# First expert's rows taken from a one-hot of ranks, second expert at a fixed place

## The chip, the cores and the metric

The kernel runs on one core of one Trainium2 chip, in float32 throughout. The metric is the device time of one execution in microseconds (us), the median of several. In the text PE is TensorE, DVE is VectorE, ACT is ScalarE, POOL is GpSimd and SP is SyncE, which issues most of the DMAs.

## The reference

One step of a hybrid decoder layer: 256 prompt rows and 32 sample rows, 288 in all, of width 2048, pass a mixer (gated MLP heads beside sparse attention), a cross-attention into 256 memory tokens, and a mixture of experts. The change is in the last part only:

```python
def hier_moe(n, w_group, b_group, w_router, b_router, w_gate, w_up, w_down):
    xf = n.reshape(B * T, D)
    g_prob = softmax(xf @ w_group + b_group); g_sel = argmax(g_prob)        # 4 groups
    e_logits = (xf @ w_router + b_router) ... [g_sel]                       # 4 experts in the group
    top_w, top_i = lax.top_k(softmax(e_logits), 2)
    top_w = top_w / sum(top_w) * g_gate
    expert_id = g_sel * 4 + top_i
    for e in range(16):
        h = silu(xf @ w_gate[e]) * (xf @ w_up[e])                           # 2048 -> 512
        y = y + combine[:, e:e + 1] * (h @ w_down[e])                       # 512 -> 2048
```

Routed on the reference's inputs, 288 rows pick 576 experts: 21 21 21 19 44 37 50 69 33 36 56 47 28 24 39 31 rows for experts 0 to 15.

## The kernel before, in words

The mixer and the attention take the first 740 us or so. Then the router's logits are computed, the rows are routed, and the experts run one after another.

**Lots and ring.** An expert's weights are six lots of 2.10 MB (128 partitions x 4096 floats): gate and up for the first half of the contraction, gate and up for the second, and two halves of down. The 16 experts make 96 lots, here numbered 0 to 95. They lie in a ring of nine buffers (`ring_at`). SP issues lot n once the semaphore `moe_free` says n + 1: the first nine places come free as earlier stages leave their memory (increments of PE at L1158 to L1220), each later one when PE has read the lot that lies there. PE adds two after the first half of gate and up (products 0 to 7 of 16), two after the second half, and one after each half of down. So lots 9 and 10 wait for the first half of the first expert's gate products.

**Order of the experts.** The expert at place 0 is always expert 0. The others are ranked by how many rows they got (`rnk`, L2313 to L2316): ten take full blocks of 64 rows (`CAP`), the fullest gets a strip of 32 rows more, and the five least filled are light and have 32 rows (`STRIP`) each. Whatever does not fit goes to overflow blocks behind the last expert, which load their expert's six lots again. The order is known when `hot_ready` is 3; SP waits for it ahead of lot 6 (L543) and reads the expert's number from `ids_order`.

**From the router to the first expert.** PE turns the normed rows back (L1210), ACT lays them in `hx` (L1871), POOL writes them to DRAM (`nsc`, L622). PE sums the picks to ranks and counts (L1216, L1218), DVE works out block and place of each pick (L2313 to L2341) and two one-hots (`blk_hot`, `row_hot`), PE multiplies these to tables of slots (`slot_table`, L1227, once for the row numbers and once for weights and scales), DVE turns the first into row addresses (`tabS`), POOL gathers block 0 from DRAM by them (L629), PE turns it (`rows_t`, L1244), DVE lays it as `XT` (`lay_rows`, L2392), and the gate products start (L1292). While it waits, PE does products that nobody reads (`keep_clock`, L1233). SP also holds lot 7 until block 0 has been gathered. Block p + 1 is gathered into the other of two buffers and turned right behind the gate products of expert p.

**One full expert on PE:** 32 gate and up products (64 records in the trace, since each float32 product is two), silu on ACT (L1882), its product with the up half on DVE (L2417), a turn (L1367), a copy on ACT (L1887), 16 down products (L1374), and between them the products that put the expert before back to its rows (`combine`, L1253 and L1257).

Of the kernel before, what the change touches and what calls it, by code (L numbers as in the profile page):

```python
# [37 lines left out]
NEARLY = 2  # L38
NFULL = NEXP - NLIGHT
# [79 lines left out]
def decode_step(nc, consts, buckets, x_prompt, x_sample, cache_k, cache_v, cache_idx_k, cache_mem_k,  # L119
# [5 lines left out]
    with ctx:  # L125
# [316 lines left out]
        row_hot = SQ[:, 0:6 * CAP].rearrange("p (n r) -> p n r", n=6)  # L442
        blk_tab = SQ[:, 6 * CAP:6 * (CAP + 3 * NBLK)].rearrange("p (n b) -> p n b", n=6)
# [28 lines left out]
        fuller = pairs[:, 64:64 + 225].rearrange("p (e f) -> p e f", e=15)  # L472
# [35 lines left out]
        def _(sp):  # L508
# [31 lines left out]
            for e in range(NEXP):  # L540
                expert = e
                if e == 1:
                    sp.wait_ge(S("hot_ready"), 3)  # L543
                if e:
                    expert = sp.value_load(ids_order[:, e:e + 1], min_val=0, max_val=NEXP - 1)
                for i, (wv, part) in enumerate(LOTS):
                    lot = NL * e + i
                    sp.wait_ge(S("moe_free"), lot + 1)
                    if lot == 4:
                        sp.wait_ge(S("stored_mv0"), 16)  # L550
                    if lot == 7:
                        sp.wait_ge(S("xg_in0"), 16)
                    sp.dma_start(ring_at[lot % NRING], lot_of(wv, expert, part)).then_inc(S(f"moe_in{lot % NRING}"), 16)
# [20 lines left out]
        def _(pool):  # L574
# [71 lines left out]
        def _(pe):  # L646
# [568 lines left out]
            for at, lhs, a, z in ((0, "rank", 0, 48), (16, "ones", 0, 32), (32, "ones", 0, 16)):  # L1215
                mm(PS[:, 5, at:at + z - a], cc(lhs), AS[:, :, :].rearrange("p t e -> p (t e)")[:, a:z], start=at == 0, stop=at == 32)  # L1216
            for t in range(3):
                last = mm(PS[:, 5, 48:64], cc("ones"), AS[:, t, :], start=t == 0, stop=t == 2)  # L1218
            last.then_inc(S("rank_ready"), 1)
            pe.nop().then_inc(S("moe_free"), 2)  # L1220
# [157 lines left out]
            def down(landed, bank=4):  # L1378

                for q in range(2):  # L1380
                    w = landed(4 + q).rearrange("p (f n) -> p f n", f=2)
# [31 lines left out]
            def block_rows_t(b):  # L1413

                pe.wait_ge(S(f"xg_in{b % 2}"), 16 * (b // 2 + 1))
                if b:
                    pe.wait_ge(S("xt_laid"), b)
                rows_t(b % 2).then_inc(S("xt_ready"), 1)

            keep_clock(5)  # L1420
            block_rows_t(0)
            def gap(p):

                return lambda s: combine_step(COMBINED_IN[p], s) if p in COMBINED_IN and s < 4 else None
            for p in range(NEXP):
# [75 lines left out]
        def _(act):  # L1501
# [374 lines left out]
            A(RX, RX, ACT.Exp).then_inc(S("r_exp"), 1)  # L1876

# [60 lines left out]
        def _(dve):  # L1938
# [323 lines left out]
            own(V.memset(small[:, 352:416], 0.0))  # L2262
            own(TT(sooner, bc(cc("iota_e")[:, 0:4], 1, [128, 4, 4]), bc(cc("iota_e")[:, 0:4], 2, [128, 4, 4]), ALU.is_lt))
# [46 lines left out]
            dve.wait_ge(S("rank_ready"), 1)  # L2310
# [3 lines left out]
            each = [128, 15, 15]  # L2314
            own(TT(fuller, bc(fill[:, 1:16], 1, each), bc(fill[:, 1:16], 2, each), ALU.is_gt))
            own(V.tensor_reduce(rnk[:, 1:16], fuller, AXX, ALU.add))  # L2316
            own(TS(s32[:, 1:16], rnk[:, 1:16], 0.0, float(STRIP), ALU.is_equal, ALU.mult))
            own(TS(l32[:, 1:16], rnk[:, 1:16], float(NFULL - 1), float(CAP - STRIP), ALU.is_ge, ALU.mult))
            own(TS(later[:, 1:16], rnk[:, 1:16], float(PSTAR), float(CAP + STRIP), ALU.is_ge, ALU.mult))
# [21 lines left out]
            own(TS(ids_slot, ids_slot, CAP - 1, None, ALU.bitwise_and))  # L2341
            own(TT(blk_hot, bc(cc("iota_r")[:, 0:NBLK], 1, [128, 6, NBLK]), bc(ids_blk, 2, [128, 6, NBLK]), ALU.is_equal))
# [5 lines left out]
            by_token(blk_tok, cc("tok")).then_inc(S("hot_ready"), 1)  # L2348
# [9 lines left out]
            dve.wait_ge(S("tab_sum"), 1)  # L2358
            own(TS(tabS[:, :], PS[:, 7, 0:NBLK], 2.0, cc("half"), ALU.mult, ALU.add))
            V.tensor_copy(tabF[:, 0:NBLK], PS[:, 7, 0:NBLK]).then_inc(S("tab_ready"), 1)  # L2360
# [4 lines left out]
            dve.wait_ge(S("tab_sum"), 2)  # L2365
            own(V.tensor_copy(tabF[:, NBLK:3 * NBLK], PS[:, 4, 0:2 * NBLK]))
# [154 lines left out]
```

## Time and profile before

| | us |
|---|---|
| median of 3 runs | 1245.52 (1244.75 to 1247.62) |
| span of the profiled execution | 1242.8 |
| PE busy in it | 1162.2 (94%) |
| DVE busy | 471.6 (38%) |
| ACT busy | 192.8 (16%) |
| mean rate of the DMAs | 264 GB/s over the span |

The profiled execution is one of its own, beside the three that were timed; the page gives its span, from the first to the last instruction. That is 2.7 us under the median of the timed runs, which also hold what lies around the span. A busy PE is not PE at its peak: matmuls are pipelined, and they run at either of two granted clocks, 1.00 (2.4 GHz) and 0.50 (1.2 GHz).

### The profile page before, as it was taken

To read this page: it belongs to the slowest core of one execution; us is meant where nothing else is said; L and a number is where in the kernel's file an instruction comes from. 1 tells how busy PE (TensorE), PEld (TensorE's weight loads), DVE (VectorE), ACT (ScalarE), POOL (GpSimd) and SP (SyncE) were. 2 spreads that over 40 slices of the span, in tenths; PEclk is the share of its full clock that TensorE was granted. 3 is DMA by queue.
4 is the path that set the end of the run, shared out by engine and by line. 5 is a ranking of instruction groups with operands and counts; after the bars stand their busy time and mean duration, and the time that the engine had idled before them with its cause. 6 is when DMAs were issued, how large, how long until landed. Compare 5 with 4: busy or idle time off the path is not lost.

```text
span 1242.8 us, 14135 instructions
## 1 busy us (share of the span) xinstructions
PE 1162.2 (94%) x5878; PEld 569.7 (46%) x5878; DVE 471.6 (38%) x963; ACT 192.8 (16%) x405; POOL 49.6 (4%) x64
## 2 busy tenths in 40 slices
PE   7999999899999998999999899999999999869975
PEld 4334343344444455577777565333333333333332
DVE  5000166079745655011112465233333333412342
ACT  2112233300122234100012422000000000000000
POOL 0002000000000013100001001000000000000000
PEclk9999999999999999899999998999999999979897
DMA  8835532445333348853345636999999999999995
GB/s 288 305 125 144 154 102 87 152 151 179 123 123 102 107 155 321 321 164 136 136 159 187 269 123 251 422 428 425 428 425 427 426 427 428 425 427 428 425 428 220
DMA packets 71229, 327.85 MB, mean 264 GB/s; under 512 B 14108, under 2 KB 17980, under 8 KB 54588
## 3 DMA queue, kind: packets, MB, share of 16 engines
q1 hardware_dynamic: 55152, 282.65, 57.9%
q0 software_dynamic: 8032, 37.23, 8.0%
q10 hardware_dynamic: 7980, 7.05, 2.3%
q8 instruction: 48, 0.79, 0.3%
q14 instruction: 17, 0.14, 0.0%
HBM read 319.04 MB, written 10.49 MB: 265 GB/s over the span
## 4 chain that ended last, share of the span: by engine, by line
PE 79%; DVE 9%; DMA 6%; ACT 3%; ACTq 1%; issue 1%; DVEq 0%; SPq 0%
PE PS L712 20%; PE PS L1019 15%; PE PS L1292 13%; PE PS L1374 6%; DMA ring<-in_w_up 5%; PE PS L1253 4%; PE PS L685 3%; PE PS L1299 2%; DVE X L2038 2%; DVE top L2037 2%; PE PS L1351 1%; PE PS L830 1%; PE PS L1257 1%; PE PS L1003 1%; PE PS L1367 1%
## 5 line engine op out<-in xcount | busy, mean ns | idle before, releaser
L712 PE MATMUL PS<-ring,NC 128*128 128x512 f32 x704 | 322.6, 603 | 1.6 <-issue 1.6
L712 PEld LDWEIGHTS PS<-ring,NC 128*128 128x128 f32 x704 | 129.3, 192 | 154.4 <-issue 152.8
L1019 PE MATMUL PS<-NC,ring 128*128 128x288 f32 x768 | 189.9, 407 | 1.6 <-DVE X L2195 0.5
L1292 PE MATMUL PS<-ring,NC 128*64 128x512 f32 x560 | 163.4, 605 | 8.6 <-DMA ring<-in_w_up 7.2
L1019 PEld LDWEIGHTS PS<-NC,ring 128*128 128x128 f32 x768 | 144.6, 190 | 42.4 <-issue 2.1
L2378 DVE TENSOR_TENSOR X<-X,PS 128x1024 f32<-128x1024 f32 x52 | 63.5, 1221 | 119.2 <-PE PS L1253 119.2
L1292 PEld LDWEIGHTS PS<-ring,NC 128*64 128x64 f32 x560 | 46.3, 138 | 102.4 <-issue 100.8
L1253 PE MATMUL PS<-XNN,NC 64*128 64x512 f32 x208 | 59.0, 644 | 1.4 <-DVE XNN L2422 0.8
L1882 ACT ACTIVATE NC<-PS,small 64x512 f32<-64x512 f32 x11 | 7.5, 682 | 306.7 <-PE PS L1292 272.7
L1299 PE MATMUL PS<-ring,NC 128*32 128x256 f32 x384 | 37.2, 455 | 16.8 <-DMA ring<-in_w_up 13.3
L2195 DVE TENSOR_TENSOR X<-X,PS 128x288 f32<-128x288 f32 x16 | 7.3, 454 | 117.5 <-PE PS L1019 117.5
L2037 DVE MAX8 top<-X 32x8 f32<-32x1028 f32 (+2 forms) x48 | 44.7, 931 | 1.0
L2038 DVE MATCH_REPLACE8 X<-top,X 32x1028 f32<-32x1028 f32 (+2 forms) x48 | 43.9, 914 | 0.0
L2381 DVE TENSOR_TENSOR X<-X,PS 32x1024 f32<-32x1024 f32 x26 | 31.5, 1210 | 26.7 <-PE PS L1257 26.6
L2064 DVE TENSOR_TENSOR ring<-small,cst 64x256 f32<-64x256 f32 x1 | 0.4, 417 | 102.8 <-ACT small L1613 102.8
L1374 PE MATMUL PS<-ring,NC 128*64 128x512 f32 x176 | 39.3, 594 | 0.0
L685 PE MATMUL PS<-ring,NC 128*32 128x512 f32 x288 | 38.4, 605 | 0.0
L1299 PEld LDWEIGHTS PS<-ring,NC 128*32 128x32 f32 x384 | 18.6, 129 | 35.8 <-issue 31.5
L1253 PEld LDWEIGHTS PS<-XNN,NC 64*128 64x128 f32 x208 | 15.9, 187 | 39.5 <-issue 25.6
L2422 DVE COPY XNN<-PS 128x1024 f32<-128x1024 f32 x11 | 13.5, 1225 | 49.8 <-PE PS L1374 37.2
L2417 DVE SCALAR_TENSOR_TENSOR NC<-PS,small,NC 64x512 f32<-64x512 f32 x11 | 8.3, 756 | 50.9 <-ACT NC L1882 50.9
L629 POOL DMA_INDIRECT NC<-nsc,tabS x14 | 14.0, 998 | 340.2 <-PE PS L1244 295.4
(447 smaller groups left out, 1229.1 us busy)
## 6 DMA issues: line engine op xcount, KB each, us to landing
ring<-in_w_gate SPq DMA_DIRECT2D x27, 2048.0 KB, 22.8
ring<-in_w_up SPq DMA_DIRECT2D x22, 2048.0 KB, 20.7
ring<-in_w_in SPq DMA_DIRECT2D x36, 1024.0 KB, 5.1
ring<-in_w_down SPq DMA_DIRECT2D x16, 2048.0 KB, 21.2
ring<-in_w_out SPq DMA_DIRECT2D x16, 1024.0 KB, 5.0
nine<-in_w_down SPq DMA_DIRECT2D x6, 2048.0 KB, 25.6
XNN<-in_w_up SPq DMA_DIRECT2D x5, 2048.0 KB, 22.3
NC<-in_w_gate SPq DMA_DIRECT2D x5, 2048.0 KB, 23.7
```

The source lines that it names most:

```text
L629: nc.gpsimd.indirect_dma_start(xg[:, buf, :], None, nsc.rearrange("t (h d) -> (t h) d", h=2), bass.IndirectOffsetOnAxis(ap=tabS[:, b:b + 1 ...
L685: last = mm(acc(n, 2)[32 * k:32 * k + 32, 0:width], lhs[:, 4 * q + k, T:NT], ws[:, k, 0:width], start=st, stop=sp_)
L712: last = mm(acc(n, t)[:, 0:width], lhs[:, kt, t * 128:(t + 1) * 128], slot(m)[:, k, 0:width], start=kt == 0, stop=kt == KT - 1)
L1019: last = mm(PS[:, j, 0:NT], slot(m)[:, k, 128 * j:128 * j + 128], src[:, kt, :], start=kt == 0, stop=kt == width * 4 - 1)
L1253: last = mm(PS[:, banks + half, :], slot_w[rows, k, 128 * t:128 * t + 128], ysb[rows, k, 512 * x:512 * x + 512], start=True, stop=True)
L1292: last = mm(PS[64 * half:64 * half + 64, 2, :], x[:, kt % 8, kt // 8, :], weights[half][:, kt % 8, :], start=kt == 0, stop=kt == KT - 1)
L1299: last = mm(PS[32 * c:32 * c + 32, bank, 0:256], x[:, kt % 8, kt // 8, STRIP * sub:STRIP * sub + STRIP], weights[c // 2][:, kt % 8, 256 * ...
L1374: last = mm(PS[64 * half:64 * half + 64, bank + x, :], hT[:, f, :], w[:, f % 2, half * 1024 + x * 512:half * 1024 + x * 512 + 512], start= ...
L2037: own(V.max(best, work))
L2038: own(V.match_replace(work, best, work, TAKEN))
L2378: return TT(out, out, PS[:, banks:banks + 2, :], ALU.add)
L2381: last = TT(out, out, PS[32 * x:32 * x + 32, banks:banks + 2, :], ALU.add)
```

## The change

Block 0 is no longer gathered. As soon as the ranks are there, DVE compares each row's rank in expert 0 with 0 to 63 (`hot0`; rows not routed to expert 0 get a rank of 512 or more), and PE multiplies this one-hot with the rows in `hx`: 12 products of 512 columns. ACT copies the result to `xg`, and it is turned and laid as a gathered block was. The tables of slots are built in one pass of 66 columns, inside the gate products of expert 0, ahead of product 8. Block 1 is gathered from these tables and turned between the two halves of expert 0's down products. Expert 1 always has place 1 (`NFIXED`), 14 experts are ranked, and SP waits for the order ahead of lot 12 in place of lot 6. The wait ahead of lot 7 is gone.

```diff
+NFIXED = 2
@@ sync
-                if e == 1:
+                if e == NFIXED:
                     sp.wait_ge(S("hot_ready"), 3)
-                if e:
+                if e >= NFIXED:
                     expert = sp.value_load(ids_order[:, e:e + 1], min_val=0, max_val=NEXP - 1)
-                    if lot == 7:
-                        sp.wait_ge(S("xg_in0"), 16)
@@ gpsimd
-            for b in range(NBK):
-                if b == 1:
-                    pool.wait_ge(S("xg_in0"), 16)
+            for b in range(1, NBK):
                 if b >= 2:
                     pool.wait_ge(S("xt_ready"), b - 1)
                 block_rows(b, b % 2, f"xg_in{b % 2}")
@@ tensor
-            keep_clock(8)
-            pe.wait_ge(S("hot_ready"), 1)
-            slot_table(7, 0, NBLK).then_inc(S("tab_sum"), 1)
-            pe.wait_ge(S("hot_ready"), 2)
-            slot_table(4, NBLK, 3 * NBLK).then_inc(S("tab_sum"), 1)
+            pe.wait_ge(S("row_out"), 12)
+            pe.wait_ge(S("hot_ready"), 1)
+            for x in range(2):
+                for t in range(3):
+                    for half in range(2):
+                        at = half * 1024 + x * 512
+                        last = mm(PS[64 * half:64 * half + 64, 2 + x, :], hot0[0:ROWS[t], t, :], hx[0:ROWS[t], t, at:at + 512],
+                                  start=t == 0, stop=t == 2)
+                last.then_inc(S("route_sum"), 1)
+            keep_clock(1)
...
-            keep_clock(5)
             block_rows_t(0)
+            keep_clock(1)
+            def tables(s):
+                if s == 2:
+                    pe.wait_ge(S("hot_ready"), 2)
+                    slot_table(7, 0, 3 * NBLK).then_inc(S("route_sum"), 1)
...
                     gate_up(lots_at(p), gap(p))
-                    block_rows_t(p + 1)
+                    if p:
+                        block_rows_t(p + 1)
...
-                    down(lots_at(p))
+                    down(lots_at(p), between=(lambda: None) if p else (lambda: block_rows_t(1)))
@@ scalar
             A(RX, RX, ACT.Exp).then_inc(S("r_exp"), 1)
+            for x in range(2):
+                act.wait_ge(S("route_sum"), x + 2)
+                A(xg[:, 0, 512 * x:512 * x + 512], PS[:, 2 + x, :], ACT.Copy).then_inc(S("row_out"), 1)
+            act.wait_ge(S("tab_ready"), 2)
@@ vector
+            own(TS(passed0, AS[:, :, 0], -float(EMPTY), float(EMPTY), ALU.mult, ALU.add))
+            dve.wait_ge(S("route_sum"), 1)
+            own(TT(rank0, rank[:, :, 0], passed0, ALU.add))
+            TT(hot0, bc(cc("iota_r"), 1, [128, 3, CAP]), bc(rank0, 2, [128, 3, CAP]), ALU.is_equal).then_inc(S("hot_ready"), 1)
...
+            own(STT(rnk[:, ranked], rnk[:, ranked], 0.0, rnk[:, ranked], ALU.is_gt, ALU.add))
...
             own(TS(ids_slot, ids_slot, CAP - 1, None, ALU.bitwise_and))
+            dve.wait_ge(S("xt_ready"), 1)
+            lay_rows().then_inc(S("xt_laid"), 1)
             own(TT(blk_hot, ...))
...
+            dve.wait_ge(S("route_sum"), 4)
+            TS(tabS[:, :], PS[:, 7, 0:NBLK], 2.0, cc("half"), ALU.mult, ALU.add).then_inc(S("tab_ready"), 1)
+            V.tensor_copy(tabF, PS[:, 7, 0:3 * NBLK]).then_inc(S("tab_ready"), 1)
```

The instructions of PE from the ranks to the second half of expert 0's down products, before (x8 and the like count instructions of one shape):

```order
L1218 MATMUL PS<-mkT,cst 128x16 x3
L1233 MATMUL PS<-cst 128x512 x8
L1227 MATMUL PS<-SQ 64x22 x12
L1227 MATMUL PS<-SQ 64x44 x12
L1233 MATMUL PS<-cst 128x512 x5
L1244 MATMUL PS<-cst,NC 128x128 x8
L1292 MATMUL PS<-ring,NC 64x512 x32
L1244 MATMUL PS<-cst,NC 128x128 x8
L1367 MATMUL PS<-cst,NC 128x64 x4
L1374 MATMUL PS<-nine,NC 64x512 x8
L1374 MATMUL PS<-ring,NC 64x512 x8
```

and the same stretch of the changed kernel (its L1231, L1225, L1247, L1295, L1370 and L1377 are the L1233, L1227, L1244, L1292, L1367 and L1374 of before):

```order
L1217 MATMUL PS<-mkT,cst 128x16 x3
L1238 MATMUL PS<-X,natS 64x512 x12
L1231 MATMUL PS<-cst 128x512
L1247 MATMUL PS<-cst,NC 128x128 x8
L1231 MATMUL PS<-cst 128x512
L1295 MATMUL PS<-ring,NC 64x512 x16
L1225 MATMUL PS<-SQ 64x66 x12
L1295 MATMUL PS<-ring,NC 64x512 x16
L1370 MATMUL PS<-cst,NC 128x64 x4
L1377 MATMUL PS<-nine,NC 64x512 x8
L1247 MATMUL PS<-cst,NC 128x128 x8
L1377 MATMUL PS<-ring,NC 64x512 x8
```

The 24 table products left the place ahead of the first turn, 12 wider ones stand in the middle of the gate products, and the turn of block 1 went from ahead of L1367 into the down products.

SP's issues of lots 5 to 12, before:

```order
L553 DMA ring<-in_w_down 128x4096 [waits moe_free]
L545 TENSOR_LOAD ids [waits hot_ready]
L545 ISA x2
L553 ISA [waits moe_free]
L553 DMA ring<-in_w_gate 128x4096
L553 DMA XNN<-in_w_up 128x4096 [waits xg_in0,moe_free]
L553 ISA [waits moe_free]
L553 DMA NC<-in_w_gate 128x4096
L553 DMA ring<-in_w_up 128x4096 [waits moe_free]
```

and of the changed kernel:

```order
L553 DMA ring<-in_w_down 128x4096 [waits moe_free]
L553 DMA ring<-in_w_gate 128x4096 [waits moe_free]
L553 DMA XNN<-in_w_up 128x4096 [waits moe_free]
L553 DMA NC<-in_w_gate 128x4096 [waits moe_free]
L553 DMA ring<-in_w_up 128x4096 [waits moe_free]
L553 DMA ring<-in_w_down 128x4096 [waits moe_free] x2
L547 TENSOR_LOAD ids [waits hot_ready]
```

The load of the order moved from ahead of lot 6 to behind lot 11, and lots 6 to 8 wait for nothing but their buffers.

ACT behind its exponential, before:

```order
L1876 ACTIVATE mkT<-mkT 128x15 [waits r_shifted]
L1882 ACT_TABLE_LOAD
L1882 ACTIVATE NC<-PS,small 64x512 [waits moe_free]
L1887 ACTIVATE NC<-PS 128x256 [waits ht_ready]
L1882 ACTIVATE NC<-PS,small 64x512 [waits moe_free]
```

and of the changed kernel:

```order
L1893 ACTIVATE mkT<-mkT 128x15 [waits r_shifted]
L1896 ACTIVATE NC<-PS 128x512 [waits route_sum] x2
L1903 ACT_TABLE_LOAD [waits moe_free]
L1903 ACTIVATE NC<-PS,small 64x512 [waits tab_ready]
L1908 ACTIVATE NC<-PS 128x256 [waits ht_ready]
```

Two copies came in, and the load of the silu's table now carries the wait for `moe_free` that the silu carried.

## Rows read from the trace of the kernel before

**Rows 1.** The page's slices: GB/s that the DMAs moved, 40 slices of the span.
```profile
GB/s 288 305 125 144 154 102 87 152 151 179 123 123 102 107 155 321 321 164 136 136 159 187 269 123 251 422 428 425 428 425 427 426 427 428 425 427 428 425 428 220
```

**Rows 2.** Chain that ended last, around the twelfth expert: start, us, what.
```profile
1081.82 36.03 DMA ring<-in_w_up
...
1117.99 3.68 PE PS L1292 x8
```

**Rows 3.** Stages: us, each engine's busy time (instructions), PEclk, DMA share, GB/s.
```profile
743.00:755.00 12.00, 12.00 (x86) 9.60 (x86) 9.68 (x42) 7.77 (x15) 1.59 (x3) 1.00 1.01 382
755.00:766.60 11.60, 10.06 (x55) 6.97 (x54) 7.30 (x33) 0.00 (x0) 1.08 (x1) 0.73 0.04 10
766.60:784.00 17.40, 15.98 (x59) 6.94 (x61) 4.83 (x19) 0.00 (x0) 2.00 (x2) 0.88 0.99 404
784.00:790.00 6.00, 6.00 (x29) 2.02 (x26) 0.00 (x0) 0.15 (x1) 0.00 (x0) 1.00 0.99 400
...
829.00:858.00 29.00, 28.85 (x136) 10.00 (x134) 10.85 (x10) 1.06 (x2) 1.00 (x1) 1.00 1.01 427
```

**Rows 4.** SP's issues in order of time: lots 5, 6, 9, 15 and 21.
```profile
742.10 0.33 SPq L553 DMA_DIRECT2D ring<-in_w_down  x1
...
766.06 0.36 SPq L553 DMA_DIRECT2D ring<-in_w_gate  x1
...
782.93 0.33 SPq L553 DMA_DIRECT2D ring<-in_w_up  x1
...
809.27 0.33 SPq L553 DMA_DIRECT2D ring<-in_w_up  x1
...
838.47 0.33 SPq L553 DMA_DIRECT2D ring<-in_w_up  x1
```

**Rows 5.** Instructions from the router to the first expert: start, us, engine, line, shapes.
```profile
744.54 5.46 PE L1210 MATMUL PS<-cst,XNN 128*128 128x128 f32 x48
...
745.23 5.86 ACT L1871 ACTIVATE X<-PS 128x512 f32<-128x512 f32 x12 [1.65 <-PE PS L1210]
...
750.51 0.82 PE L1218 MATMUL PS<-mkT,cst 128*128 128x16 f32 x6
...
751.37 0.17 DVE L2313 SCALAR_TENSOR_TENSOR mkT<-PS,cst 128x16 f32<-128x16 f32 x1
...
751.58 0.39 DVE L2315 TENSOR_TENSOR mkT<-mkT 128x225 f32<-128x225 f32 x1
751.59 1.28 ACT L1882 ACT_TABLE_LOAD   x1
...
758.36 0.17 DVE L2341 TENSOR_SCALAR ids<-ids 128x6 int32<-128x6 int32 x1
...
759.84 7.08 PE L1227 MATMUL PS<-SQ 128*64 128x22 f32 x48 [1.54 <-DVE SQ L2347]
...
764.65 1.08 POOL L629 DMA_INDIRECT NC<-nsc,tabS  x1 [12.74 <-issue]
...
773.12 1.28 PE L1244 MATMUL PS<-cst,NC 128*128 128x128 f32 x9
774.54 1.23 DVE L2392 TENSOR_TENSOR NC<-PS,gcol 128x1024 f32<-128x1024 f32 x1 [7.39 <-PE PS L1244]
...
775.82 13.95 PE L1292 MATMUL PS<-ring,NC 128*64 128x512 f32 x64 [1.42 <-DVE NC L2392]
```

**Rows 6.** ACT and PE behind the first gate products, columns as in rows 5.
```profile
789.85 0.68 ACT L1882 ACTIVATE NC<-PS,small 64x512 f32<-64x512 f32 x1 [36.98 <-PE PS L1292]
...
792.87 3.65 PE L1374 MATMUL PS<-nine,NC 128*64 128x512 f32 x16 [0.47 <-ACT NC L1887]
```

**Rows 7.** Stages around the table products, columns as in rows 3.
```profile
759.80:760.80 1.00, 0.96 (x10) 0.90 (x10) 0.86 (x5) 0.00 (x0) 0.00 (x0) 0.82 0.00 0
...
766.80:770.40 3.60, 3.60 (x6) 1.51 (x5) 0.20 (x1) 0.00 (x0) 1.01 (x1) 0.50 1.00 336
```

**Rows 8.** The 14 gathers of blocks: us from issue to landing.
```profile
DMA to landing us min/median/max: 3.4/10.7/12.0
```

More of the change, by code:

```diff
@@ L1215, in _ @@
             for at, lhs, a, z in ((0, "rank", 0, 48), (16, "ones", 0, 32), (32, "ones", 0, 16)):
-                mm(PS[:, 5, at:at + z - a], cc(lhs), AS[:, :, :].rearrange("p t e -> p (t e)")[:, a:z], start=at == 0, stop=at == 32)
+                last = mm(PS[:, 5, at:at + z - a], cc(lhs), AS[:, :, :].rearrange("p t e -> p (t e)")[:, a:z], start=at == 0, stop=at == 32)
+            last.then_inc(S("moe_free"), 2)
             for t in range(3):
                 last = mm(PS[:, 5, 48:64], cc("ones"), AS[:, t, :], start=t == 0, stop=t == 2)
-            last.then_inc(S("rank_ready"), 1)
-            pe.nop().then_inc(S("moe_free"), 2)
+            last.then_inc(S("route_sum"), 1)
             def slot_table(bank, a, z):
@@ L1233, in keep_clock @@
                     mm(PS[:, 6, :], ident, cst[:, 128:640], start=True, stop=True)
-            keep_clock(8)
+            pe.wait_ge(S("row_out"), 12)
             pe.wait_ge(S("hot_ready"), 1)
-            slot_table(7, 0, NBLK).then_inc(S("tab_sum"), 1)
-            pe.wait_ge(S("hot_ready"), 2)
-            slot_table(4, NBLK, 3 * NBLK).then_inc(S("tab_sum"), 1)
+            for x in range(2):
[4 more added lines that the diff above has]
+                                  start=t == 0, stop=t == 2)
+                last.then_inc(S("route_sum"), 1)
+            keep_clock(1)
             def rows_t(k):
@@ L1376, in down_products, with down @@
                 return last
-            def down(landed, bank=4):
+            def down(landed, bank=4, between=lambda: None):
                 for q in range(2):
+                    if q:
+                        between()
                     w = landed(4 + q).rearrange("p (f n) -> p f n", f=2)
@@ L1413, in block_rows_t @@
             def block_rows_t(b):
-                pe.wait_ge(S(f"xg_in{b % 2}"), 16 * (b // 2 + 1))
                 if b:
+                    pe.wait_ge(S(f"xg_in{b % 2}"), 16 * ((b + 1) // 2))
                     pe.wait_ge(S("xt_laid"), b)
+                else:
+                    pe.wait_ge(S("row_out"), 14)
                 rows_t(b % 2).then_inc(S("xt_ready"), 1)
-            keep_clock(5)
             block_rows_t(0)
+            keep_clock(1)
[3 more added lines that the diff above has]
+                    slot_table(7, 0, 3 * NBLK).then_inc(S("route_sum"), 1)
             def gap(p):
+                if p == 0:
+                    return tables
                 return lambda s: combine_step(COMBINED_IN[p], s) if p in COMBINED_IN and s < 4 else None
@@ L2262, in _ @@
             own(V.memset(small[:, 352:416], 0.0))
+            own(V.memset(rnk[:, 1:NFIXED], 1.0))
             own(TT(sooner, bc(cc("iota_e")[:, 0:4], 1, [128, 4, 4]), bc(cc("iota_e")[:, 0:4], 2, [128, 4, 4]), ALU.is_lt))
@@ L2308, in _ @@
             TT(RX[:, :, 0:4], LG[:, :, 0:4], bc(r_max, 2, [128, 3, 4]), ALU.subtract).then_inc(S("r_shifted"), 1)
-            dve.wait_ge(S("rank_ready"), 1)
+            own(TS(passed0, AS[:, :, 0], -float(EMPTY), float(EMPTY), ALU.mult, ALU.add))
+            dve.wait_ge(S("route_sum"), 1)
             rank = PS[:, 5, 0:48].rearrange("p (t e) -> p t e", t=3)
             count = PS[:, 5, 48:64]
+            own(TT(rank0, rank[:, :, 0], passed0, ALU.add))
+            TT(hot0, bc(cc("iota_r"), 1, [128, 3, CAP]), bc(rank0, 2, [128, 3, CAP]), ALU.is_equal).then_inc(S("hot_ready"), 1)
             own(STT(fill, count, 32.0, cc("iota_e"), ALU.mult, ALU.add))
[L2314 to L2319, printed above, removed]
+            ranked, each = slice(NFIXED, NEXP), [128, NEXP - NFIXED, NEXP - NFIXED]
+            own(TT(fuller, bc(fill[:, ranked], 1, each), bc(fill[:, ranked], 2, each), ALU.is_gt))
+            own(V.tensor_reduce(rnk[:, ranked], fuller, AXX, ALU.add))
+            own(STT(rnk[:, ranked], rnk[:, ranked], 0.0, rnk[:, ranked], ALU.is_gt, ALU.add))
+            own(TS(s32[:, ranked], rnk[:, ranked], 0.0, float(STRIP), ALU.is_equal, ALU.mult))
+            own(TS(l32[:, ranked], rnk[:, ranked], float(NFULL - 1), float(CAP - STRIP), ALU.is_ge, ALU.mult))
+            own(TS(later[:, ranked], rnk[:, ranked], float(PSTAR), float(CAP + STRIP), ALU.is_ge, ALU.mult))
             own(STT(limit, s32, float(CAP), l32, ALU.add, ALU.subtract))
@@ L2347, in by_token @@
                 return TT(per_pick(out), per_pick(blk_hot), ap.unsqueeze(1).unsqueeze(3).broadcast_to(x), ALU.mult)
-            by_token(blk_tok, cc("tok")).then_inc(S("hot_ready"), 1)
+            own(by_token(blk_tok, cc("tok")))
             own(by_token(blk_rs, xrs))
@@ L2357, in _ @@
             own(STT(at_place, s32[0:1, :], PSTAR / STRIP, at_place, ALU.mult, ALU.add))
-            dve.wait_ge(S("tab_sum"), 1)
-            own(TS(tabS[:, :], PS[:, 7, 0:NBLK], 2.0, cc("half"), ALU.mult, ALU.add))
-            V.tensor_copy(tabF[:, 0:NBLK], PS[:, 7, 0:NBLK]).then_inc(S("tab_ready"), 1)
             own(TT(who, bc(at_place, 1, [1, 16, 16]), bc(cc("iota_e", 1), 2, [1, 16, 16]), ALU.is_equal))
@@ L2364, in _ @@
             V.tensor_copy(ids_order, at_place).then_inc(S("hot_ready"), 1)
-            dve.wait_ge(S("tab_sum"), 2)
-            own(V.tensor_copy(tabF[:, NBLK:3 * NBLK], PS[:, 4, 0:2 * NBLK]))
+            dve.wait_ge(S("route_sum"), 4)
+            TS(tabS[:, :], PS[:, 7, 0:NBLK], 2.0, cc("half"), ALU.mult, ALU.add).then_inc(S("tab_ready"), 1)
+            V.tensor_copy(tabF, PS[:, 7, 0:3 * NBLK]).then_inc(S("tab_ready"), 1)
+            dve.wait_ge(S("tab_ready"), 2)
             dve.wait_ge(S("iota_in"), 16)
```

11 lines of the change are left out of this document (5 added, 6 removed).

## The prediction

> **What bounds the kernel now.** I read the slices first, then the chain that ended last, then the stages, then SP's issues, and single instructions last. In the slices the last third is level at 425 to 428 GB/s [rows 1]: while the experts run, the DMAs are full. The chain says the same from the other side: at the first strip expert it goes through a weight lot issued at 1081.82 that PE could use only 36 us later [rows 2]. Yet in the full experts PE has no gap either: 28.85 of 29.00 us [rows 3]. Both are near their limit there. SP's issues for one lot of successive experts are 29.2 us apart (809.27 and 838.47) [rows 4], while six lots of 2.10 MB with some 0.4 MB of gathered rows take 13.0 / 0.427 = 30.4 us at the rate of that stage [rows 3]. So PE runs ahead by 1.2 us per expert until the ring is empty of landed lots, and what sets the end is when the stream of lots gets going and how often it stops. An idle DMA before the last lot counts one for one; an idle PE counts only if it starves the stream of free buffers.
>
> The stream has a hole: 11.6 us at 10 GB/s from 755.0 to 766.6 [rows 3]. It ends with lot 6 at 766.06 [rows 4], the first that waits for the order of experts. Behind it the rate is 404 and 400 GB/s up to 790 [rows 3], and from there on full. The changed kernel closes this hole. The question is whether buffers come free in time, since lots 9 to 15 need the gate and down products of expert 0 and the start of expert 1.
>
> **Part 1, the start of the gate products.** Ranks and counts are summed at 750.51 + 0.82 = 751.33, and the gate products start at 775.82 [rows 5]. In place of this: DVE does one small operation ahead of the wait, one behind it (0.17 each, 0.2 with the gap) and the one-hot of 192 elements, by the 0.39 of L2315's 225 [rows 5]: 752.2. The 12 products with 64 weight columns are 24 records; 64 such records took 13.95 us, 0.218 each [rows 5], so 5.2: 757.4. ACT's second copy is a twelfth of 5.86, 0.5 [rows 5]: 757.95. One idle product, by four of those records 0.9, hides it: 758.3. The turn is 1.3 [rows 5]: 759.6. DVE must by then be through with ids_slot: it was at 758.53 [rows 5], and three small operations and the one-hot add 1.0, which gives 759.5, just in time; every 0.1 more there is 0.1 on the path. XT is laid in 1.23 [rows 5], so the gate products start at 761.0, 14.8 us earlier.
>
> **Part 2, expert 0 on PE.** Half of the gate products, 7.0, are done at 768.0. The table pass is 24 records: ten of them took 0.96 us while the clock was still mostly high [rows 7], 48 took 7.08 mostly at the low clock [rows 5]; that is 2.3 to 3.5, and I take 2.4, as PE is warm there. It needs the one-hots, some 2.7 us of DVE behind XT, about 763.7, and is hidden; the order of experts follows at about 765.7 and is needed by SP for lot 12 at 777. The gate products end at 761.0 + 13.95 + 2.4 = 777.35. Now the silu's table: its load took 1.28 at 751.59, with ACT idle [rows 5]. In the changed order this load carries the wait for `moe_free`, so it stands behind the gate products: +1.3 (nothing, if the load gets ahead after all). From the end of the gate products to the down products it was 792.87 - 789.77 = 3.1 [rows 5, 6]: 781.75. The turn of block 1 no longer fills this time, so PE idles 2.9 us there. An idle time of 1.54 ahead of L1227 [rows 5] was followed by a fall of the granted clock, and then 3.6 us of wide products at 0.50 [rows 7]. So I charge the first down half 3.5 + 2.0 (bounds 0 and 3.5): 787.25. The turn of block 1 costs 1.4 in the open, the second half 3.5: expert 1 starts at 792.15, against 792.87 + 7.0 = 799.9, 7.8 earlier. Of the 14.8 us PE gives back 2.4 to tables, 1.3 to the silu's table, 2.0 to the clock, 1.4 to the turn.
>
> Block 1's gather: tables are summed at 768.0 + 2.4 = 770.4, DVE and POOL bring the issue to about 772, the median gather lands 10.7 later and the slowest 12.0 [rows 8]: 782.7 to 784. It is needed at 787.25, or at 785.2 without the fall of the clock. It waits for nothing else, as block 2 uses the other buffer.
>
> **Part 3, the stream.** From 743 to 755 the DMAs moved 4.58 MB [rows 3]: lot 5, the rows written to `nsc` (2.36 MB) and a little; at 427 that is 10.7 us, so starting costs up to 1.3. The changed kernel issues lots 5 and 6 at 742.1 to 742.5 and 7 and 8 at 751: with them 10.9 MB, 25.5 us from 744.3, so 769.8. Lots 9 and 10 are issued at 768.0, in time: with two gathers (21 rows for expert 1, 0.8 us for both) 780.4. Lots 11 and 12, issued at 777.4: 790.2. Lot 13, issued at 787.25: 795.1. Lot 14, at 792.15, and a gather: 800.9. Lot 15 needs the first half of expert 1, which took 809.27 - 799.9 = 9.3 [rows 4, 6]: issued at 801.5. The stream runs dry here; with 1.5 us from issue to full flow (0.9 to 2.2) lot 15 begins at 803.0. From there each expert brings DMA 1.2 us more than PE needs, and it stays full.
>
> Before, lot 15 began after lots 6 to 14 and three gathers, 19.6 MB or 46.0 us from 766.6, plus 0.9 and 0.4 for the two stages below 427 [rows 3]: 813.9. The difference is 10.9 us, and behind lot 15 both kernels move the same lots. The other edits cost nothing: the memset stands ahead of the router beside PE's products, one tensor_scalar fewer ranks 14 in place of 15, SP has one load of the order less.
>
> The Trainium skill, "DMA: Bandwidth & Descriptors", section Specifications, gives about 0.6 us to the first byte for DMAs that SP issues. By that the restart at lot 15 would be 0.9 us shorter, and the time 0.9 lower; the row of 743 to 755 gives more, and I follow the row.
>
> **The sum.** Against its own execution: span 1242.8 - 10.9 = 1231.9; the median of the timed runs lies 2.7 above that span, so 1245.5 - 10.9 = **1234.6**. Own range: at best neither the silu's table nor the clock costs, lot 15 is issued at 798.2, and the full stream sets its start at 799.9 to 801.0: 14.0 gained, 1231.5. At worst within the mechanism, the dear table pass (1.1), the dear clock (1.5) and the slow restart (0.7): 1237.9.
>
> **Rivals.** (a) *The clock falls ahead of the first rows.* PE waits 0.9 us for the one-hot behind narrow products and then runs wide ones. The 24 records at half speed cost between 1.8 (3.6 us at 0.50, as behind L1227 [rows 7]) and 5.2; lot 15 is later by as much: 1236.4 to 1239.8. Against it: from 743 to 755, turns and narrow products included, the clock was 1.00 [rows 3]. The Trainium skill speaks for it ("TensorE: Matmul & The Clock Gate", Part 4: transposes do not count as PE-busy in the same way, so 5.46 us of them would leave the clock low). The trace disagrees so far, as the products right behind them ran at 1.00.
> (b) *PE becomes the bound.* If PE and not the stream sets the end, only its 7.8 us arrive: 1237.7. For it: no gap in the full experts. Against it: the 36 us wait [rows 2].
> (c) *A new wait on the gather.* In the changed kernel six lots are queued when block 1 is gathered. If it lands 16 to 20 us after its issue, PE and lot 14 are late by 1 to 5: 1236 to 1239. No gather took over 12.0 [rows 8].
> (d) *An overflow block: slower.* With expert 1 fixed at a full block, the five light ones are the least filled of 2 to 15, so expert 15 comes in, with 31 rows by the reference's inputs against a strip of 32. From 33 rows on there is an overflow block: six lots more, 6 x 4.9 = 29.5 us, behind the last expert, with nothing beside them: 1264. The counts speak against it.
> (e) *The hole was free anyway.* If the rate late in the stream falls by what comes earlier, nothing is gained. Only the level 425 to 428 speaks, and against it.
>
> **How the numbers follow.** Forecast 0.60, (a) 0.20, (b) 0.07, (c) 0.05, (d) 0.03, (e) 0.05. What this kernel's measurement can tell from no change is 0.2%, 2.5 us, so faster means under 1243.0. Forecast, (a), (b) and (c) lie there: 0.92; (e) is no change, with 0.04 of its 0.05; (d) and the rest slower: 0.04. The range of 8 in 10 takes the forecast's and reaches through (a) to (c): 1231.0 to 1240.0.
>
> **What would show it.** Right, if the gate products start at 760 to 762; if the rate holds near 427 from 744 to 770 with no stretch under 50 GB/s; if ACT's table load stands behind 777 with 2.5 to 3 us of PE idle and a half clock in the first down products; if the second expert's gate products start near 792; and if lot 15 is issued near 801.5 after a short dip. Wrong, if the hole only moves (lots 9 and 10 issued past 772), if the gather releases the turn of block 1, or if the wait at the first strip expert is gone, since then PE sets the end.

## The result, and the profile after

The changed kernel took 1237.82 us (median of 5, 1233.77 to 1239.22) against 1245.52 (also of 5, 1244.75 to 1247.62). The medians lie 7.7 us apart; the ratio is 0.9922 with a 95% interval of 0.9902 to 0.9942, so 7 to 12 us were gained. The forecast was a gain of 10.9 us and a time of 1234.6. In the profiled execution the span was 1236.5 and the time 1239.10.

The first thing to see in that trace is that lot 5 is issued at 747.09 and not at 742.10 as before [rows 4], though nothing ahead of it was changed but one small memset. Here are SP's issues in the changed kernel (start, us, what; lots 5 to 10 and 15, the pair 10 and 11 in one row):

```profile
747.09 0.33 SPq L553 DMA_DIRECT2D ring<-in_w_down  x1
747.46 0.43 SPq L553 DMA_DIRECT2D ring<-in_w_gate  x1
...
755.70 0.33 SPq L553 DMA_DIRECT2D XNN<-in_w_up  x1
756.07 0.65 SPq L553 DMA_DIRECT2D NC<-in_w_gate  x1
773.70 0.33 SPq L553 DMA_DIRECT2D ring<-in_w_up  x1
774.07 9.35 SPq L553 DMA_DIRECT2D ring<-in_w_down  x2
...
807.83 0.33 SPq L553 DMA_DIRECT2D ring<-in_w_up  x1
```

So I count from the issue of lot 5. T is the time from there to the end of the span: 1242.8 - 742.1 = 500.7 before, 1236.5 - 747.1 = 489.4 after. Lot 9 went from 40.8 behind lot 5 to 26.6, lot 15 from 67.2 to 60.7, the last lot, 95, from 454.5 to 445.0. PE is 6.5 us earlier at lot 15, the stream of lots 9.5 us earlier at its end, and the tail behind the last issue is 1.8 shorter (44.4 in place of 46.2). That makes T 11.3 shorter.

The tail's part has nothing to do with the stream: the last expert's down products ran at the full clock in this trace and in part at the half clock before (start, us; the first two rows are of the changed kernel, the last two of the kernel before):

```profile
1220.06 1.92 PE L1354 MATMUL PS<-nine,NC 128*32 128x512 f32 x16 [0.48 <-ACT NC L1913]
1221.77 1.93 PE L1354 MATMUL PS<-ring,NC 128*32 128x512 f32 x16
...
1224.84 3.50 PE L1351 MATMUL PS<-nine,NC 128*32 128x512 f32 x16 [0.43 <-ACT NC L1892]
1228.15 1.91 PE L1351 MATMUL PS<-ring,NC 128*32 128x512 f32 x16
```

That is 1.6 of the 1.8 us.

The stages of the changed kernel (us, each engine's busy time, PEclk, DMA share, GB/s) answer to [rows 3]:

```profile
760.00:765.00 5.00, 5.00 (x25) 2.32 (x24) 3.62 (x18) 1.19 (x2) 0.00 (x0) 1.00 1.02 431
785.00:790.00 5.00, 3.51 (x11) 1.65 (x13) 0.76 (x1) 0.55 (x2) 0.00 (x0) 0.53 1.00 422
795.00:805.00 10.00, 10.00 (x44) 2.87 (x43) 3.64 (x3) 0.00 (x0) 0.99 (x1) 1.00 0.99 415
805.00:810.00 5.00, 5.00 (x24) 1.56 (x24) 2.31 (x2) 0.00 (x0) 0.00 (x0) 1.00 0.82 311
810.00:829.00 19.00, 18.85 (x94) 7.08 (x90) 7.32 (x8) 1.06 (x2) 0.99 (x1) 1.00 0.97 393
829.00:858.00 29.00, 28.85 (x135) 10.01 (x134) 10.66 (x10) 1.06 (x2) 0.99 (x1) 1.00 1.01 429
```

The hole is gone: 431 GB/s where it had been. Ahead of that, while the rows' write to DRAM was on its way, the rate was not near 427 as forecast but 340 GB/s from 747 to 755 and 375 to 760. What is left is a shortfall around lot 15, where the forecast had the stream run dry: against 427 GB/s the rows from 795 to 829 lack 0.3, 1.4 and 1.5 us (length times the missing share). Most of the last 1.5 is a second, smaller dip right behind the issues of lots 17 and 18 (817.25 and 818.35), with 1.2 us missing:

```profile
818.00:824.00 6.00, 5.85 (x34) 2.58 (x35) 3.82 (x4) 0.38 (x1) 0.99 (x1) 1.00 0.90 340
```

The clock is at 0.53 from 785 to 790, where PE had waited for the silu.

The instructions of the route answer to [rows 5, 6] (start, us, engine, line, shapes, idle before):

```profile
757.14 5.81 PE L1238 MATMUL PS<-X,natS 128*64 128x512 f32 x24 [0.81 <-DVE natS L2337]
...
763.85 1.32 PE L1247 MATMUL PS<-cst,NC 128*128 128x128 f32 x9
...
765.31 1.23 DVE L2370 TENSOR_TENSOR NC<-PS,gcol 128x1024 f32<-128x1024 f32 x1 [1.10 <-PE PS L1247]
...
766.59 7.09 PE L1295 MATMUL PS<-ring,NC 128*64 128x512 f32 x32 [0.56 <-DVE NC L2370]
...
773.51 2.55 PE L1225 MATMUL PS<-SQ 128*64 128x66 f32 x24
...
783.19 1.28 ACT L1903 ACT_TABLE_LOAD   x1 [19.59 <-PE PS L1295]
...
786.01 1.07 PE L1370 MATMUL PS<-cst,NC 64*128 64x64 f32 x5 [2.94 <-DVE NC L2442]
...
787.56 5.92 PE L1377 MATMUL PS<-nine,NC 128*64 128x512 f32 x16 [0.47 <-ACT NC L1908]
```

The reader is to see the silu's table loaded behind the gate products, the 2.94 us of idle PE that follow, and the first down half at 5.92 us in place of 3.65 [rows 6].

The chain that ended last still waits for a lot at the first strip expert, as in [rows 2]:

```profile
1078.73 35.20 DMA ring<-in_w_up
```

### The profile page after: what moved, and what is told of

Same layout as the page of the kernel before. It is cut to its first block, busy times and chain, and to the rows that moved or that the text cites. A ratio compares the mean times of both kernels' runs of the same rounds, so it can differ in the third digit from the quotient of the medians.

```text
span 1236.5 us, 14083 instructions
## 1 busy us (share of the span) xinstructions
PE 1153.0 (93%) x5856; PEld 561.8 (45%) x5856; DVE 472.6 (38%) x967; ACT 194.1 (16%) x407; POOL 48.7 (4%) x63
## 4 chain that ended last, share of the span: by engine, by line
PE 79%; DVE 8%; DMA 6%; ACT 3%; ACTq 2%; issue 1%; DVEq 0%
PE PS L710 20%; PE PS L1017 15%; PE PS L1295 13%; PE PS L1377 7%; DMA ring<-in_w_up 5%; PE PS L1256 4%; PE PS L683 3%; PE PS L1302 2%; DVE X L2059 2%; DVE top L2058 2%; PE PS L828 1%; PE PS L1260 1%; PE PS L1370 1%; PE PS L1001 1%; DMA NC<-in_cache_v,ids 1%
## 5 line engine op out<-in xcount | busy, mean ns | idle before, releaser
L1295 PE MATMUL PS<-ring,NC 128*64 128x512 f32 x560 | 163.7, 605 | 9.0 <-DMA ring<-in_w_up 8.4
L1295 PEld LDWEIGHTS PS<-ring,NC 128*64 128x64 f32 x560 | 46.3, 138 | 103.6 <-issue 102.2
L1302 PE MATMUL PS<-ring,NC 128*32 128x256 f32 x384 | 33.9, 425 | 16.1 <-DMA ring<-in_w_up 14.0
L2412 DVE TENSOR_TENSOR X<-X,PS 32x1024 f32<-32x1024 f32 x26 | 31.5, 1210 | 26.6 <-PE PS L1260 26.4
L1377 PE MATMUL PS<-ring,NC 128*64 128x512 f32 x176 | 39.4, 595 | 0.0
L1824 ACT ACTIVATE NC<-X,gcol 128x288 f32<-128x288 f32 x16 | 8.6, 535 | 117.0 <-DVE X L2216 117.0
```

Source lines behind the costliest of these rows:

```text
L1295: last = mm(PS[64 * half:64 * half + 64, 2, :], x[:, kt % 8, kt // 8, :], weights[half][:, kt % 8, :], start=kt == 0, stop=kt == KT - 1)
L1302: last = mm(PS[32 * c:32 * c + 32, bank, 0:256], x[:, kt % 8, kt // 8, STRIP * sub:STRIP * sub + STRIP], weights[c // 2][:, kt % 8, 256 * ...
L1377: last = mm(PS[64 * half:64 * half + 64, bank + x, :], hT[:, f, :], w[:, f % 2, half * 1024 + x * 512:half * 1024 + x * 512 + 512], start= ...
L2412: last = TT(out, out, PS[32 * x:32 * x + 32, banks:banks + 2, :], ALU.add)
```

## The experiments

Each timed run is given as the ratio to the kernel before on the same chip, with its 95% interval. The medians of the kernel before in the three sets were 1246.83, 1246.87 and 1248.51.

**The two kernels again.** Both unchanged, for more traces.

> The kernel before once more, unchanged, for a second trace. T is the time from the issue of lot 5 to the end of the span: 1242.8 - 742.1 = 500.7 in the first trace of before, 1236.5 - 747.1 = 489.4 in that of after. Theory (the stage of routing and experts is nearly fixed, and what ran ahead of lot 5's issue varies from execution to execution by some us, with falls of the granted clock and small waits): T is 500.7 within 1 us, and lot 5 is issued anywhere from 741 to 748. Rival (the change itself delays the work ahead of lot 5, by 5 us): lot 5 is issued at 742.1 within 1 us here, and in every trace of before.

> The changed kernel once more, unchanged. Theory: T is 489.4 within 1 us; lot 5 is issued anywhere from 741 to 748; timed, the mean gain lies between 8 and 11 us. Rival (the change delays what runs ahead of lot 5): lot 5 at 747.1 within 1 us again, and the timed gain is 6.3 in every round.

> The changed kernel a third time, as the measure for clock_kept_2 on the same chip. Theory: T 488.5 to 490, lot 15 issued 60.7 behind lot 5, median 7 to 11 us under before.

before_again: lot 5 at 743.50, T 499.8 (one run, 1245.19). after_again: lot 5 at 743.86, T 488.9, ratio 0.9930 (0.9906 to 0.9954). after_third: lot 5 at 741.94, T 489.7, ratio 0.9934 (0.9907 to 0.9962). Lot 15 stands 60.7 to 60.9 behind lot 5 in all three traces of the changed kernel. So the 5 us ahead of lot 5 were not the change's: over all 14 traces taken, lot 5's issue lies between 739.2 and 747.3. It goes with the granted clock ahead of it. By the clock's records in each trace, the granted clock was 0.50 for 10 us in total where lot 5 came at 739.2, for 17 to 24 us in the nine traces where it came at 741.9 to 743.9, and for 27 to 31 us in the four where it came at 746.6 to 747.3. One piece shows when the two first traces are laid side by side: at 242 us the products of L830 (L828 in the changed kernel) took 3.42 us in place of 1.90 and the next 16 products 9.78 in place of 8.80, with the same code and the same 1.60 us of idle PE between the two groups. Why the clock falls in one execution and not in another stays open.

The medians differ by 7.9 and 8.2 us, as 7.7 in the first measurement, where T says 11; within the intervals, but three times on the same side.

**One half of the change without the other.** rows_only is the changed kernel with the order of experts awaited ahead of lot 6 as before:

```diff
-NFIXED = 2
+NFIXED = 1
...
-            own(V.memset(rnk[:, 1:NFIXED], 1.0))
...
-            own(STT(rnk[:, ranked], rnk[:, ranked], 0.0, rnk[:, ranked], ALU.is_gt, ALU.add))
```

> The changed kernel with only expert 0 fixed, so that 15 experts are ranked as before and lot 6 waits for their order. Theory (the stream sets the end): the order is ready about 1 us later behind lot 5 than before (it now stands behind the laying of block 0), so the hole stays and ends at lot 6, some 25 us behind lot 5; from there the stream is full without its two weaker stages (0.9 and 0.4 us) and without block 0's gather (0.4): T is 499.5 to 501, little or nothing gained, though PE is 6 to 8 us earlier at expert 1. Rival (PE sets the end): PE's lead at expert 1 arrives at the end: T 493 to 495.

fixed_only is the kernel before with NFIXED = 2, the wait ahead of lot 7 deleted, and `moe_free` raised by the last rank product, in place of a nop that stood behind the products of the counts.

> The kernel before with the second expert at the fixed place two and without the wait for block 0 ahead of lot 7; block 0 is still gathered, the tables stand ahead of the gate products. Theory (the stream of lots sets the end, and a buffer must come free for it to go on): lots 6 to 8 move into the hole of 11.6 us, but lot 9 is still issued 40.8 us behind lot 5 when the first half of the gate products is done, so the hole only moves to behind lot 8; T is 500.7 less 0 to 1 us, the median within 1.5 us of before. Rival 1 (each us of idle DMA that is filled is gained by itself): T near 490. Rival 2 (PE sets the end): T 500.7, as PE does the same at the same time; this run does not tell it from the theory.

fixed_wait7 puts that wait back:

```diff
+                    if lot == 7:
+                        sp.wait_ge(S("xg_in0"), 16)
```

> The kernel before with the second expert fixed (as in fixed_only), but with the wait for block 0 ahead of lot 7 put back, so that only lots 5 and 6 are in flight beside the write of the rows to DRAM. In fixed_only the gather of block 0 was issued at 774.95, 7.3 us behind its table, released by the landing of that write. Theory (lots 7 and 8 share the DMAs with this write and delay it, and with it the gather, the gate products and lot 9): here the gather follows its table by 1.2 to 3 us, and the median is within 1.5 us of before, 3 to 5 us under fixed_only. Rival (the fixed place itself costs, by the ranks of DVE or the order of experts): the median stays 4 us above before.

rows_only: ratio 1.000 (0.998 to 1.0019), nothing gained, though lot 9 was issued 29.6 and lot 15 64.2 behind lot 5 (before 40.8 and 67.2). The hole stayed: lot 6 was issued 27.8 behind lot 5. The bound by PE falls with this run. In its trace T was 504.3 and not 499.5 to 501. A fall of the clock at the router, which the forecast did not hold, has 3.1 us of it: two short groups of products took 0.7 us more, and the 48 turned records behind them 7.90 in place of 5.46 [rows 5]. Without it T would be about 501.2. PE's lead was there all the same, as lot 15 came 3 us earlier than before in spite of the fall. The rows of the turned records and of lot 6:

```profile
749.99 7.90 PE L1208 MATMUL PS<-cst,XNN 128*128 128x128 f32 x48
...
774.72 0.36 SPq L553 DMA_DIRECT2D ring<-in_w_gate  x1
```

fixed_only: ratio 1.0043 (1.002 to 1.0066), slower than before by 4.0 us in the medians and 5.4 by the ratio, where 0 to 1 us less was expected. T was 504.5. Lots 6 to 8 did fill the hole, and lot 9 came 44.6 behind lot 5, not 40.8. Its trace has the reason in POOL's row for the gather of block 0 (first fixed_only, then fixed_wait7):

```profile
767.66 0.24 DVE L2360 TENSOR_SCALAR tabS<-PS,cst 128x22 uint32<-128x22 f32 x1 [1.51 <-PE PS L1226]
...
774.95 1.08 POOL L628 DMA_INDIRECT NC<-nsc,tabS  x1 [18.58 <-DMA nsc<-X]
...
763.63 0.24 DVE L2362 TENSOR_SCALAR tabS<-PS,cst 128x22 uint32<-128x22 f32 x1 [1.82 <-PE PS L1228]
...
765.07 1.08 POOL L630 DMA_INDIRECT NC<-nsc,tabS  x1 [12.87 <-issue]
```

The gather follows its table by 7.3 us (1.4 before: 764.65 against 763.2), and was released by the landing of the rows' write to DRAM. With the wait back this is gone: in fixed_wait7 the table is written at 763.63 and the gather issued at 765.07, T is 500.8, the ratio 1.0003 (0.9981 to 1.0025; it overlaps that of fixed_only by a hair). So fixing the place costs nothing that these runs can tell, and the wait on the write comes with lots 7 and 8.

What fixed_only's 4 to 5 us are made of is less clean. In this trace too the clock had fallen at the router (48 turned records in 8.03 us), so the write was issued 2.9 later behind lot 5; the wait for its landing adds 5.9 (7.3 - 1.4); and 4.9 come back, as the gather now finds the DMA engines empty and the gate products start 6.3 us behind its issue in place of 11.2. The sum is 3.9 us, and lot 9 is 3.8 late. The wait on the write is thus shown, but in the trace it nets about 1 us beside the router's 2.9; how much of the timed 4 to 5 us is its own stays open. The Trainium skill, "DMA: Bandwidth & Descriptors", section "Queues, rings and completion order", says that each DMA engine takes packets in turn from the queues that have work. The traces agree. In fixed_only the write was issued from 751.42 to 755.85, with lots 5 to 8 on SP's queue, and its last part landed 18.2 us behind its issue; with lots 5 and 6 beside it (fixed_wait7) this took 10.3 us, with lot 5 alone (before) 5.1.

In the changed kernel it is as long, 19.0 us: issued at 756.38, landed at 775.41. There nobody waits for it, but only because the tables were ready 0.9 later, at 776.34. By these rows a route to the tables that is faster by more than that would meet this wait; no run tests it.

So the fixed place gains nothing alone, and without the wait at lot 7 it loses; the one-hot of rows gains nothing alone; and both together gain 8 us in the medians and 11 in T.

**What is left behind the first gate products.** silu_early and clock_kept each take one cost of the forecast away, both_kept both (with two unread products in place of three):

```diff
# silu_early, ACT behind the two row copies
+            own(A(sg[0:1, 0:1], cst[0:1, 0:1], ACT.Silu))
# clock_kept, PE behind the gate products
                     if p:
                         block_rows_t(p + 1)
+                    else:
+                        keep_clock(3)
```

> The changed kernel with one silu of a single element on ACT behind the two row copies, so that the silu's table is loaded while ACT is idle; all else as in the change. T is again the time from lot 5's issue to the end; 489.4 and 488.9 in the two traces of the changed kernel, with lot 15 issued 60.7 behind lot 5 in both. Theory (behind the gate products of expert 0 PE's time sets when buffers come free, and the stream of lots runs nearly dry around lots 14 to 16): the table's 1.28 us leave the path, lot 15 is issued 59.4 behind lot 5, T 487.5 to 488.3. Rival (the stream is fed well enough, these waits are off the path): lot 15 earlier by 1.3 all the same, T 489.2 as before.

> The changed kernel with three products that nobody reads (128x512) right behind the gate products of expert 0, in the 2.9 us in which PE waits for the silu; all else as in the change. Theory (the fall of the granted clock to 0.50 comes from this idle time and costs 5.92 - 3.58 = 2.3 us in the first down half): no fall, the 16 records of the first down half take 3.6 us, lot 15 is issued 58.4 behind lot 5, T 486.5 to 487.5. Rival 1 (the clock falls for what came before, table products among it): still 5 to 6 us there. Rival 2 (off the path): clock kept, T 489.2.

> Both of the last two edits (with two unread products in place of three, since the wait is then 1.6 us). Theory: lot 15 is issued 57.1 behind lot 5, but the stream has only some 2.9 us of shortfall to give back between 795 and 829 in the trace of the changed kernel (1.4 from 805 to 810, 1.5 from 810 to 829), so T is 486 to 487 and not 485.6, and the timed median is 2 to 3 us under the changed kernel's. Rival: T 489.2, nothing gained.

> clock_kept once more, beside the changed kernel. Theory: T 486.4 within 1 us; the median is 2 to 3.5 us under after_third's. Rival (the 7 us between the medians of clock_kept and of the changed kernel, taken in different calls, are real): 6 to 8 us under it.

| | lot 15 behind lot 5 | lot 95 behind lot 5 | T | median | ratio to before |
|---|---|---|---|---|---|
| after, after_again, after_third | 60.7, 60.7, 60.9 | 445.0, 443.9, 445.3 | 489.4, 488.9, 489.7 | 1237.82, 1238.96, 1240.34 | 0.9922, 0.9930, 0.9934 |
| silu_early | 60.1 | 444.2 | 491.1 | 1235.80 | 0.9889 (0.985 to 0.9929) |
| clock_kept | 58.4 | 442.0 | 486.4 | 1231.01 | 0.9858 (0.9827 to 0.9889) |
| both_kept | 57.3 | 442.1 | 486.6 | 1236.32 | 0.9906 (0.9877 to 0.9936) |
| clock_kept_2 | 61.4 | 444.9 | 490.7 | 1236.31 | 0.9908 (0.9881 to 0.9935) |

clock_kept's first down half, behind products that keep PE busy:

```profile
779.78 2.84 PE L1231 MATMUL PS<-cst 128*128 128x512 f32 x6
...
782.79 1.02 PE L1370 MATMUL PS<-cst,NC 64*128 64x64 f32 x5 [0.17 <-DVE NC L2444]
784.28 3.65 PE L1377 MATMUL PS<-nine,NC 128*64 128x512 f32 x16 [0.47 <-ACT NC L1910]
```

3.65 us in place of 5.92, and so in all four traces with the idle time filled: it is what let the clock fall, and lot 15 is 2.3 earlier. In silu_early PE still idles 1.68 us ahead of L1370, and the first down half is 0.6 longer still, which eats half of the table's 1.28. That need not be the shorter idle time's doing, as with 2.94 us it took 5.92 in one trace and 6.44 in another (rows_only):

```profile
782.07 6.52 PE L1377 MATMUL PS<-nine,NC 128*64 128x512 f32 x16 [0.47 <-ACT NC L1909]
```

T missed its forecast of 487.5 to 488.3, at 491.1; 2.4 of that lie behind the last issue, where the tail was 46.9 against 44.4 (1.5 of them the half clock in the last down products again). both_kept is 1.1 us ahead of clock_kept at lot 15 and level with it at lot 95: beyond clock_kept there is nothing to gain here, as the stream is nearly full. Its stages show it, against the same three stretches of the changed kernel:

```profile
795.00:805.00 10.00, 10.00 (x46) 2.72 (x44) 3.33 (x3) 0.00 (x0) 0.00 (x0) 1.00 1.01 424
805.00:810.00 5.00, 5.00 (x22) 1.45 (x24) 2.43 (x3) 0.00 (x0) 0.00 (x0) 1.00 1.00 406
810.00:829.00 19.00, 18.85 (x94) 7.08 (x90) 7.20 (x8) 1.06 (x2) 0.99 (x1) 1.00 1.01 426
```

clock_kept was run twice. Beside the changed kernel on one chip it was 4.0 us under it (1236.31 against 1240.34), with intervals that overlap. Its second trace missed: T 490.7, since the clock fell at the router (8.00 us for the 48 turned records) and all from lot 7 on came 3.0 later, and the tail was 1.3 longer. Its first median, 1231.01, is the lowest seen, and its interval (up to 0.9889) the only one wholly under those of the changed kernel. But both_kept, on the same chip, with the same fall avoided and the same T, lies 5.3 us above it. So the 3.0 us in T are shown for this edit, and the rest of that median's lead is not.

**The router's idle time.** router_kept is clock_kept with one unread product ahead of `router(3)`:

```diff
+            mm(PS[:, 5, :], ident, cst[:, 128:640], start=True, stop=True)
             router(3).then_inc(S("r_sums"), 1)
```

> clock_kept with one more unread product, in the 1.1 us in which PE waits for ACT ahead of the router's last part. Behind this wait the clock fell to 0.50 in the traces of fixed_only and rows_only (48 records of turned rows in 8.03 and 7.90 us) and not in the five others of that kind (5.46). Theory (this idle time lets the clock fall in some executions): 5.46 us in the trace, T 486 to 487, the highest of the timed runs come down, the median 0 to 2 us under clock_kept_2's. Rival (the falls have another cause ahead of this place): the spread and the median stay as clock_kept_2's.

The trace had 5.46 us and T 486.7, but most traces without this product have that too. The median, 1237.65 (ratio 0.992, 0.9891 to 0.9948), is not under clock_kept_2's, and the spread is about the same (6.9 us against 6.3). Whether this idle time lets the clock fall stays open.

**The price of an overflow block.** third_fixed has `NFIXED = 3`, ranks 1 and 2 set by memset, and the operation that shifts the other ranks done twice.

> The changed kernel with experts 0, 1 and 2 at fixed places 0, 1 and 2 and 13 experts ranked. Expert 8, with 33 rows by the reference's inputs, becomes one of the five light ones with 32 rows, and one row of it goes to an overflow block. This prices rival (d) of the prediction. Theory: six lots more in a full stream cost 6 x 4.9 = 29.5 us, and the products that nothing covers some us more: median 29 to 40 us above the changed kernel's, over 15 us slower than before. Rival (the block's lots are loaded beside the light experts' products, where PE had waited for lots, and cost less): under 25 us.

1303.82 us, ratio 1.0463 (1.0427 to 1.0498): 63 us above the changed kernel, twice the theory's; T is 554.8, 65 above. The lots of the block are issued 27 us behind the last one of the ordinary stream (1183.55), when the light experts' buffers are free, and little runs beside what follows: from 1251.0 to 1275.7 the DMAs move nothing and PE is busy for 9.6 us (start, us, what, in the chain that ended last):

```profile
1209.53 0.05 SPq L559
...
1210.53 0.34 SPq L563
...
1212.16 21.22 DMA ring<-in_w_up
...
1233.51 7.11 PE PS L1295 x32
...
1250.96 1.24 DVE XNN L2504
...
1269.84 5.88 issue
1275.72 5.59 PE PS L1354 x32
```

From 1209.5 to 1275.7 are 66 us: a load of six lots that starts from an empty queue, a whole expert in series, and six steps of combining.

## Why the prediction was right, and where it was not

**What bounds the kernel: right.** The stream of lots sets the end. rows_only moved PE and not the stream and gained nothing; both_kept moved PE beyond what the stream could use, and lot 95 stayed. The wait at the first strip expert, whose loss was to be a sign of being wrong, is there (35.2 us, 36.0 before).

**Part 1, the gate products 14.8 us earlier: nearly.** They start 19.5 behind lot 5, forecast 18.9, before 33.7: 14.2 earlier. The 24 records took 5.8 and not 5.2: their starts do lie within 5.2 us, but the last one runs out its whole length of 0.59, and ACT's copy 0.6 and not 0.5. DVE was in time.

**Part 2: each step nearly as forecast.** The tables took 2.4 us (773.68 to 776.06), the silu's table 1.28, the idle time 2.94 (2.9), the clock 5.92 - 3.65 = 2.3 (2.0), the turn 1.45 (1.4). Expert 1 starts 51.3 behind lot 5, forecast 50.1: 0.6 late from part 1, 0.3 from the clock, the rest in tenths of the other steps.

**Part 3: mechanism right, two sizes off.** Lot 15 was issued 60.7 behind lot 5 (forecast 59.4), the 1.2 us of expert 1's start and 0.1 behind it. The stream did run short there: the forecast had it idle for 2.1 us, 1.5 of them the restart, where its own row of 743 to 755 gives at most 1.3; from 806 to 812 the trace lacks 1.7 us (303 GB/s). And the stream did not "stay full" behind lot 15: from 818 to 824 it lacks 1.2 us (340 GB/s), a term that the forecast had at nothing. So the stream gained 9.5 us at its last issue and not 10.9; these terms add up to somewhat more than the 1.4 us between, and the rest was not followed. With the 1.8 us of a shorter tail, which the forecast did not hold, T came out at 11.3. That this is so near 10.9 is luck: 1.6 of it is the clock in the last down products, which stood at 1.00 there in all three traces of the changed kernel but fell again in those of silu_early and clock_kept_2.

**The time itself: 3 us over the forecast, inside the range.** The forecast took its gain off the median of before, so an early or late lot 5 in one trace does not explain this; what has to be explained is that the medians differ by 8 us where T differs by 11. Three pieces can be named. The last issue of the stream gained 9.5 us, not 10.9. The tail's 1.6 us hang on a clock that falls in some executions. And the time of an execution is longer than its span by 1.8 to 1.95 us in all 54 further runs of the kernel before, but by 1.8 to 3.2 (mean 2.4) in the 20 of the changed kernel: 0.5 us that no span shows, cause unknown. Part of the rest may be the clock at the router, which costs about 3 us when it falls (3 of 14 traces), but no run shows that it falls more often in the changed kernel.

**The rivals.** (a), the clock falling ahead of the first rows, did not occur: it was 1.00 from 747 to 785 in the trace after, right behind the turned rows too. The rule of the Trainium skill that I had set beside it ("TensorE: Matmul & The Clock Gate", Part 4) is not borne out there; in the three traces with a fall at this place the turned rows were themselves already slow. (b) is refuted by rows_only. (c) did not occur: the turn of block 1 follows the down products with no wait. Its gather landed 10.5 us behind its issue, 5.6 before it was needed; the one of block 2, issued 1.4 later, took 15.2 (12.0 at most before), but is not needed until expert 1's gate products are through. (d) did not occur either, but its price was wrong by more than half: 63 us and not 29.5. (e) is refuted by the gain.

## What to carry to other kernels

When a stream of transfers sets the end, a hole in it is worth its length only if buffers come free behind it: look for the next wait of the stream before the first is removed, and expect two changes to be worth nothing apart. Transfers that fill a hole share the engines with whatever else is in flight there, and if that is on the path to the next free buffer, they cost. Where the load of a function's table takes over a wait from the instruction behind it, the order of instructions shows it, and nothing in the source does.

## What the runs showed that was not expected

The rows' write to DRAM, 2.36 MB, landed 18 us after its last issue with four lots beside it (fixed_only), 5 us with one (before), and its reader waited 5.9 us for it, where it had never been waited for. An idle time of 1.68 us was followed by a fall of the clock just as 2.94 us was (6.52 against 5.92 us for the same products), so shortening it by 1.3 us gave back half of that, and filling it kept the clock at 1.00 through the products behind it.

And identical code moved by up to 8 us ahead of lot 5 from one execution to the next, which is the size of the effect studied: only times counted from a fixed event of the same trace could tell the steps apart. The mean granted clock tells such executions apart: of the 25 timed runs of the kernel before on one chip, the shortest span, 1239.4 us, had 0.976 and the longest, 1248.4, had 0.967. Even T is not free of this: the clock in the last products moved it by 1.5 us.
